# Norms of block 2 done in two halves of rows ahead of the next stage's first groups; differential attention combining three heads back

## What is computed

```python
def second_block(x, norm_gains, w_ffn_gate, w_ffn_up, w_ffn_down, w_in, w_out, diff_lambda, diff_subln_gain):
    for layer in range(DEPTH_2):
        g = norm_gains[layer]
        h = rmsnorm(x, g[0])
        x = x + 0.5 * rmsnorm(swiglu(h, w_ffn_gate[layer, 0], w_ffn_up[layer, 0], w_ffn_down[layer, 0]), g[1])
        h = rmsnorm(x, g[2])
        x = x + rmsnorm(token_mixer_2(h, w_in[layer], w_out[layer], diff_lambda[layer], diff_subln_gain[layer], layer), g[3])
        h = rmsnorm(x, g[4])
        x = x + 0.5 * rmsnorm(swiglu(h, w_ffn_gate[layer, 1], w_ffn_up[layer, 1], w_ffn_down[layer, 1]), g[5])
    return x
```

```python
a1 = softmax(q1 @ k1.T + bias)
a2 = softmax(q2 @ k2.T + bias)
out = (a1 - lam * a2) @ v          # causal, in blocks of 128 queries
```

## Time and profile before

| | |
|---|---|
| median of three runs | 3760.9 us (3751.8 to 3766.9) |
| the profiled execution | 3745.1 us |
| its span, first to last instruction | 3743.3 us |
| mean granted TensorE clock, share of full speed | 0.935 |
| TensorE busy | 3360.8 us, 90% |
| VectorE busy | 1483.1 us, 40% |
| ScalarE busy | 1065.6 us, 28% |
| DMA queue 1, share of 16 engines | 31.5% |

### The profile page before, as it was taken

One profiled execution on the slowest core, in us unless ns is written; L12 is line 12 of the kernel. 1 busy time (PEld: TensorE's weight loads), 2 busy tenths in 40 slices (PEclk: granted clock), 3 DMA queues, 4 the chain that ended last, 5 costly groups with the idle time before them and its releaser, 6 DMA issues. The chain is left out here.

```text
span 3743.3 us, 53089 instructions
## 1 busy us (share of the span) xinstructions
PE 3360.8 (90%) x23548; PEld 2516.5 (67%) x23548; DVE 1483.1 (40%) x2077; ACT 1065.6 (28%) x1663; POOL 166.7 (4%) x167
## 2 busy tenths in 40 slices
PE   6988778887988786999998889999999998789999
PEld 5856667774543333887786468877887787468877
DVE  3345655556111115333424543334333434453333
ACT  3225433321100002222323542224222323552222
POOL 0002222121000000000000000000000000000000
PEclk8989898987989997999999699999999999799999
DMA  6140000013699996222311032223232221032221
GB/s 240 46 154 1 2 3 3 13 68 147 274 373 421 421 421 221 90 90 90 106 69 57 1 101 90 90 90 108 83 102 90 75 100 57 1 101 85 95 90 40
DMA packets 173984, 441.01 MB, mean 118 GB/s; under 512 B 5954, under 2 KB 97852, under 8 KB 149180
## 3 DMA queue, kind: packets, MB, share of 16 engines
q1 hardware_dynamic: 173756, 437.61, 31.5%
HBM read 435.49 MB, written 2.10 MB: 117 GB/s over the span
## 5 line engine op out<-in xcount | busy, mean ns | idle before, releaser
L333 PE MATMUL banks<-mix_r,ring_r 128*128 128x512 f32 x1776 | 701.8, 395 | 0.0
L333 PE MATMUL banks<-mix_r,ffn_r 128*128 128x512 f32 x1664 | 665.8, 400 | 10.9 <-ACT mix_r L2483 4.7
L333 PE MATMUL banks<-h_r,ffn_r 128*128 128x512 f32 x1664 | 651.7, 392 | 0.0
L295 DVE TENSOR_TENSOR ring_r<-ring,ffn_r 128x2048 fp32r<-128x2048 f32 (+2 forms) x168 | 357.4, 2127 | 230.8 <-ACT ffn_r L292 230.8
L292 ACT ACTIVATE ffn_r<-ring 128x2048 fp32r<-128x2048 f32 (+2 forms) x168 | 299.7, 1784 | 479.8 <-PE banks L333 473.3
L2211 PE MATMUL banks<-ring,arena 128*64 128x512 f32 x1024 | 357.3, 623 | 51.1 <-DMA arena<-in_exp_w_up 19.1
L333 PEld LDWEIGHTS banks<-mix_r,ring_r 128*128 128x128 f32 x1776 | 335.8, 189 | 83.4
L333 PEld LDWEIGHTS banks<-mix_r,ffn_r 128*128 128x128 f32 x1664 | 315.4, 190 | 80.2 <-issue 13.1
L333 PEld LDWEIGHTS banks<-h_r,ffn_r 128*128 128x128 f32 x1664 | 315.2, 189 | 73.5
L2793 PE MATMUL banks<-ring_r,ffn_r 128*128 128x512 f32 x704 | 279.2, 397 | 0.0
L2792 PE MATMUL banks<-ffn_r 128*128 128x512 f32 x640 | 253.6, 396 | 4.7 <-DVE arena L2743 4.7
(11 more groups left out here) (431 smaller groups left out, 4996.1 us busy)
## 6 DMA issues: line engine op xcount, KB each, us to landing
ring<-in_exp_w_up SPq DMA_DIRECT2D x24, 2048.0 KB, 16.3
ring<-in_exp_w_down SPq DMA_DIRECT2D x23, 2048.0 KB, 21.3
ring<-in_w_ffn_gate SPq DMA_DIRECT2D x44, 1024.0 KB, 5.4
ring<-in_w_ffn_up SPq DMA_DIRECT2D x44, 1024.0 KB, 8.0
ring<-in_w_ffn_down SPq DMA_DIRECT2D x20, 2048.0 KB, 7.7
ring<-in_w_in SPq DMA_DIRECT2D x17, 2048.0 KB, 8.3
ring<-in_exp_w_gate SPq DMA_DIRECT2D x17, 2048.0 KB, 17.6
arena<-in_exp_w_gate SPq DMA_DIRECT2D x15, 2048.0 KB, 18.6
```

Source lines behind the costliest of these rows:

```text
L295: l.did(V.tensor_tensor(lo, x_, hi, ALU.subtract).then_inc(l.sem, 1), name, "lo", v)
L333: ins = TE.matmul(m[1](bank), m[2], m[3], start=m[4], stop=m[5])
```

## The change

1. At each junction the first two groups of the next product stage are done in halves of columns. `first_half` issues them for columns 0 to 255 (row tiles 0 and 1) between the transposes of tiles 2 and 3, as soon as the low parts of tiles 0 and 1 and of the weights are there. The stage itself then does columns 256 to 511 of those two groups, behind a wait for the low parts of tiles 2 and 3, and without its fence.
2. ScalarE and VectorE do the high and low parts of tile 1 directly behind those of tile 0, ahead of the norm of tile 3.
3. The mixer's first unit is 256 columns wide, so that it carries two groups; the buffers of the later units change places.
4. Differential attention combines unit u-3 instead of u-2, has a sixth buffer, and both TensorE's and ScalarE's steps are in another order.

```diff
+                        if begun and i == 0:
+                            for t in (2, 3):
+                                l.wait_ge(*past(begun[1], "lo", t))
...
-                            if m[0] == "t":
+                            if begun and i < begun[0]:
+                                ins = TE.matmul(m[1](bank)[:, T // 2:T], m[2], m[3][:, T // 2:T], start=m[4], stop=m[5])
+                            elif m[0] == "t":
...
+            def first_half(l, name, groups, behind):
+
+                for t in (0, 1):
+                    l.wait_ge(*past(behind, "lo", t))
+                l.wait_ge(*past(name, "lo", 0))
+                for i, g in enumerate(groups):
+                    for m in g["mms"]:
+                        TE.matmul(m[1](banks[:, i, :])[:, 0:T // 2], m[2], m[3][:, 0:T // 2], start=m[4], stop=m[5])
...
                         if nset == 2:
                             if 1 <= k < N:
                                 scores(k, (1,))
+                            if k + 1 < N:
+                                scores(k + 1, (0,))
...
                         if k >= 2:
                             values(k - 2)
-                        if nset == 2 and k + 1 < N:
-                            scores(k + 1, (0,))
...
-                    for u in range(2 * N + 2):
+                    lag = 3 if nset == 2 else 2
+                    for u in range(2 * N + lag):
...
-                        if u >= 2:
-                            finish(u - 2)
+                        if u >= lag:
+                            finish(u - lag)
...
+                    if nset == 2:
+                        for k in range(N + 3):
+                            if k < N:
+                                weights(2 * k)
+                            if 1 <= k <= N:
+                                normal(2 * k - 1)
+                            if 2 <= k <= N + 1:
+                                evac(k - 2)
+                            if k >= 3:
+                                out_(k - 3)
+                            if k < N:
+                                weights(2 * k + 1)
+                                normal(2 * k)
+                        return
...
-                                if t == NT - 1:
-                                    evac(1)
                                 of_x(t)
                                 if t == NT - 2:
                                     evac(0)
+                                    evac(1)
...
                         for t in range(2 if done else 0, NT):
+                            if t == NT - 1:
+                                first_half(l, ahead[0], ahead[2], name)
                             turn_x(l, name, t)
...
-                    products(nm, gs, units=units, depth=DEPTH, presplit=1 if early else 0)
+                    products(nm, gs, units=units, depth=DEPTH, fence=False, presplit=1, begun=(2, early))
...
-                        hi = ffn_r(ytmp_at + 11264 if u == 0 else rest_end if u % 2 else extra, KD, width)
+                        hi = ffn_r(ytmp_at + 11264 if u == 0 else extra if u % 2 else rest_end, KD, width)
...
-                              ([region(extra + i * D, D) for i in range(3)] + [region(y_at_, D), region(y_at_ + D, D)],
-                               pt, stats[:, 64:104].rearrange("p (a b) -> p a b", b=8)),
+                              ([region(extra + i * D, D) for i in range(3)] + [region(y_at_ + i * D, D) for i in range(2)] + [region(hT_at + 2048, D)],
+                               pt, stats[:, 64:112].rearrange("p (a b) -> p a b", b=8)),
```

46 lines of the change are left out of this document (23 added, 23 removed).

## The result

The changed kernel takes **3700.8 us**, the median of four runs (3692.1 to 3710.5). The kernel before, in the same comparison, takes 3756.4 us (3749.8 to 3766.9, four runs). The ratio is 0.9854, with a 95% interval from 0.9829 to 0.9879. That is 45 to 64 us faster.

What follows compares the result with a forecast made beforehand. TensorE, busy 90% of the span, was taken as the bound, so only its idle or half-clock time could be won. Junctions 31.0 - opening 1.5 + attention 6.0 = 35.5 us off 3760.9: 3725 us, range 3709 to 3745.

Steps and rivals of the forecast that it cites:

- the base of 3760.9 us: Whole kernel: median of the runs shown, from which 35.5 us were taken; 15.8 us above the profiled execution's 3745.1 us.
- the 5 us left for the spread of the runs: Range's low end, 3709 us: some of the runs' own spread allowed, though runs lay 15 us apart.
- The junctions: Five junctions in block 2: half the products fill TensorE's idle time ahead of tile 3's transposes; 6.2 us each, 31.0 us.
- clock falls as before: Rival at the junctions: half clock as before, each gains only 2.6 us; 3746 us in all; chance 0.13.
- halves not at twice the rate: Rival at the junctions: each half product waits for its 0.19 us weight load; 20 us slower, 3781 us; chance 0.04.
- The clock allowance of 0.7 us per junction: Junctions: taken off 6.9 us, half of 1.5 us for some 15 products at half clock behind tile 3.
- The opening: Start of block 2: the half waits for the weights' low part and delays tile 3's transposes; loses 1.5 us.
- Attention: Two differential attention stages: gain in the first part of each, 3 us a stage, 6.0 us, bounds -7 and +12.
- that wait goes: Differential attention: VectorE's 11.3 us wait per stage ahead of combining, for ScalarE's normalising, falls to under 4 us.
- What is late next is TensorE: Differential attention, middle of the stage: TensorE busy 19.57 of 19.70 us at half clock, so nothing to win there.
- The sixth buffer only allows the lag: Differential attention: the sixth buffer's sole role is to make the lag of three possible; no size of its own.
- a largest gain of 47 us: Range's low end: junctions at 6.9 us each and attention near its upper bound of +12 us.

Runs made afterwards that it cites:

- the half done twice: Changed kernel, but the stage behind each junction does its first two groups whole again, so the half is only filling: 3738.7 us, ratio 0.9969.
- the low parts left late: Changed kernel, but tile 1's high and low parts are split inside the norm of tile 3, as before the change: 3718.7 us, ratio 0.9923.
- The lag alone: Kernel before with the lag of three and the sixth buffer, TensorE's and ScalarE's orders as before: 3747.8 us, one run.
- the two single parts: Changed kernel with attention as before: 3715.4 us, ratio 0.9909; kernel before with only the attention change: 3740.0 us, ratio 0.9981.
- the two comparisons: Changed kernel against the kernel before, measured twice without an edit: 3700.8 against 3756.4 us, ratio 0.9854; then 3705.6 against 3740.6 us, ratio 0.9897.

## Why the prediction was right, and where it was off

The result lies below the stated range. The step that put it there is the last one of the sum, the base of 3760.9 us from which the 35.5 us were taken, together with the 5 us left for the spread of the runs. The mechanism at the junctions was right, with one term of its sum too large. The mechanism given for attention was wrong.

**The junctions: right in every step.** The half begins 1.35 us behind tile 2's transposes (1.3 forecast), its products are 0.119 us apart (0.118), the transposes of tile 3 follow with no wait, and the whole comes out at 6.87 us where the clock holds. That the half costs no time but moves it is shown by the half done twice (5.4 us back). That the step on VectorE was the one to watch is shown by the low parts left late (22 us back). The rivals "clock falls as before" and "halves not at twice the rate" did not come true: with 0.119 us from start to start, the 0.19 us loads of the weights lie under the products.

**The clock allowance of 0.7 us per junction: mis-sized.** In the seven profiles with the half and with tile 1 split early the clock fell at 2 of 35 junctions, at some 1.6 us each. It is worth 0.1 us per junction, not 0.7. The five junctions gave 35 us, not 31.0. Another 1 us of this comes from taking the first junction for all: "mid0b" and "mid1b" had taken 24.3 and 24.1 us to the third group, not 23.5.

**The opening: right.** 1.6 us lost to the third group, 1.5 forecast; over the whole stretch up to "mid0a" about 1.2 us.

**Attention: the size near by luck, the reason wrong.** The step "with a lag of three, and ScalarE normalising the odd head ahead of its evacuations, that wait goes" is true (0.3 us left), but the time does not come from it, and ScalarE's new order is not needed for it. The lag alone also leaves only 0.9 us of that wait and gains nothing, since VectorE then waits 19.1 us for scores (layer 0 of that kernel) instead of 9.1. "What is late next is TensorE" was written, but only as a bound on the gain. TensorE's new order takes 19.1 down to 15.4. "The sixth buffer only allows the lag" is not so either, since the lag of three ran with five. Besides, the sum stopped at the end of the stage. The stick-breaking stage behind it moves by up to 4 us either way, with the moment at which the clock falls. Counting both stages gives 7.4 us in the mean, where the forecast had 6.0.

**The sum.** With the measured terms, the opening over its whole stretch among them: 35 - 1.2 + 7.4 = 41 us, where the forecast had 35.5. The traces give 38.2 and 41.4 us for block 2, the two single parts 34.8 + 10.1 = 45 us by the medians, and the two comparisons 55.5 and 35 us. About 41 us is what the traces show. The interval of the first comparison, 45 to 64 us, does not take it in, that of the second, 30 to 47 us, does. The ten runs of the changed kernel lie 45 us under the 51 runs of the kernel before in the mean, with a 95% interval of some 40 to 50 us, an estimate that treats the five comparisons as one. That the rest of the 55.5 us is chance fits the spread of block 1, but it is argued, not shown.

**What put the result outside the range: "I take the same 35.5 us off" the median of 3760.9 us.** That median of three runs was high, and the same three are among the four runs of the kernel before in the first comparison. The kernel before had medians of 3756.4, 3750.1, 3747.0, 3751.9 and 3740.6 us in five comparisons, 3748 us when weighted by their runs. So of the 24 us between forecast and result some 13 are the baseline, some 5.5 the sum, and 6 the runs of the changed kernel (3700.8 here, 3705.6 again). The low end allowed 5 us of "the runs' own spread" beyond a largest gain of 47 us (its terms, 34.5 - 1.5 + 12, add up to 45, not 46 or 47), although the shown runs lay 15 us apart and the profiled execution was 15.8 us off the median. Whether the runs of one kernel differ by block 1 alone is not settled. The traces show that block 1 differs by up to 23 us between profiles, with its time at half clock, and block 2 of one kernel by 0 to 3 us.

## What to carry to other kernels

Where a norm or a reduction over the last rows leaves TensorE idle ahead of the next stage, do half of that stage's first groups on the rows that are ready, and put every step that feeds this half (low parts, weight split) ahead of the norm of the last rows; the order of those feeding steps was worth more than half of the gain. In a pipeline of several engines a longer lag and the order of the engine that feeds it can gain only together: here the lag without TensorE's order gave nothing, nor did the orders without the lag. And the stage behind has to be counted too. Where a median of three is the base of a forecast, widen the range by the distance between its runs, and compare stretches of a trace rather than whole times.

## What the hardware did that was not expected

- **The clock in a stage depends on the stage ahead of it.** The stick-breaking stage, 220 matmuls in each case, takes 60.3, 63.6 or 67.6 us, depending on whether it begins at half clock and whether the clock falls again in it. With the old attention it fell in every one of six stages (three profiles), 72 us behind the start of the differential stage, for 6.8 us. Behind a differential stage shorter by 1 to 3 us it misses that fall or not, and the runs don't show a rule for which.
- **A longer wait tips the clock.** With 1.35 us of idle time ahead of the half the clock held at 33 of 35 junctions; with 4.0 to 4.2 us it fell at five of five.
- **Busy is not enough to raise it.** In the middle of the differential stage TensorE is busy 19.57 of 19.70 us at half clock, and with the lag, the sixth buffer and ScalarE's order the clock stayed at half for 68.3 us in one piece.
- **A VectorE instruction took 5.20 us instead of 1.28** while POOL's subtraction of 4.49 us ran on the same core.
- **Identical code in block 1 differs by up to 23 us from one execution to another**, half of what the whole change is worth, and the difference goes with the time at half clock.
